# Off-diagonal attention values on four 32-column tiles in a hybrid convolution and forgetting-attention layer

## The reference

```python
# q, k, v: (B, S, 8 heads, 64); c = cumsum(log_sigmoid(forget logits))
s = jnp.einsum('bqhd,bkhd->bhqk', q_blk / 8, k)
s = s + c_q[..., :, None] - c_k[:, :, None, :]
s = jnp.where(causal, s, -jnp.inf)
pr = jax.nn.softmax(s, axis=-1)
y_attn = jnp.einsum('bhqk,bkhd->bqhd', pr, v)
```

## Time and profile before

| | |
|---|---|
| median of 3 runs | 4268.29 us (4263.36 to 4269.75) |
| the profiled execution | 4270.38 us |
| its slowest core (3), first to last instruction | 4268.8 us |
| spans of its eight cores | 4252.9 to 4268.8 us |
| mean granted TensorE clock of core 3 | 0.985 of full speed |
| TensorE busy / ScalarE busy / VectorE busy | 97% / 54% / 44% of the span |

### The profile page before, as it was taken

The page is one execution under the profiler, slowest core; times in us unless marked ns, Lnnn a source line. Parts: engine busy times, 40 slices in busy tenths (PEclk is TensorE's granted clock), DMA queues, the critical chain, the costliest instruction groups (busy, mean ns, idle before and its releaser), DMA issues.

```text
span 4268.8 us, 73847 instructions; the slowest of 8 cores (4252.9 to 4268.8 us)
## 1 busy us (share of the span) xinstructions
PE 4128.3 (97%) x23192; PEld 1673.9 (39%) x23192; DVE 1873.9 (44%) x3245; ACT 2293.5 (54%) x4028; POOL 282.9 (7%) x619
## 2 busy tenths in 40 slices
PE   6999899999999999999999999999999999999978
PEld 3444343443433333333444444444333333333333
DVE  4566554353443433424444453534434344343334
ACT  3525345464666666766334354645557566676621
POOL 1111000010000000000000000101001000000000
PEclk9999999999999999999999999999999999999989
DMA  8798965463543543624556473635436354352344
GB/s 193 148 186 205 197 191 158 121 191 116 155 144 108 160 126 110 175 90 150 174 165 183 133 203 123 194 122 167 145 114 190 102 153 139 98 162 95 99 141 124
DMA packets 350372, 635.10 MB, mean 149 GB/s; under 512 B 201648, under 2 KB 206000, under 8 KB 350000
## 3 DMA queue, kind: packets, MB, share of 16 engines
q1 hardware_dynamic: 333408, 585.89, 45.6%
q0 software_dynamic: 16592, 44.51, 6.9%
HBM read 567.84 MB, written 61.87 MB: 148 GB/s over the span
## 4 chain that ended last, share of the span: by engine, by line
PE 89%; DMA 4%; ACT 2%; issue 2%; DVE 2%; POOL 1%; SPq 0%; ACTq 0%; DVEq 0%; POOLq 0%
PE ps L1143 39%; PE ps L1327 14%; PE ps L1227 12%; PE ps L980 7%; PE ps L1037 6%; PE ps L1043 3%; PE ps L1072 2%; DMA xnC<-xnbf 2%; PE ps L989 1%; PE ps L1365 1%; DMA brow_s<-brow 1%; DMA xt<-x 1%; PE ps L986 1%; PE ps L1230 1%; ACT jk L669 1%
## 5 line engine op out<-in xcount | busy, mean ns | idle before, releaser
L1008 ACT ACTIVATE P<-ps,cKb 128x512 bf16<-128x512 f32 x1792 | 1105.7, 688 | 560.4 <-PE ps L980 558.0
L1143 PE MATMUL ps<-xnC,wslot 128*128 128x512 bf16 x5632 | 1288.7, 381 | 21.8 <-DMA xnC<-xnbf 11.8
L1143 PEld LDWEIGHTS ps<-xnC,wslot 128*128 128x128 bf16 x5632 | 533.4, 98 | 688.0 <-issue 98.2
L732 DVE TENSOR_TENSOR xt<-xt,ps 128x512 f32<-128x512 f32 x512 | 351.5, 687 | 661.6 <-PE ps L1327 489.3
L1327 PE MATMUL ps<-wslot,actT 128*128 128x512 bf16 x2816 | 637.2, 379 | 0.8 <-DVE actT L1189 0.8
L1143 PE MATMUL ps<-xnA,wslot 128*128 128x512 bf16 x2560 | 613.2, 389 | 0.3 <-DVE wslot L574 0.3
L1183 DVE SCALAR_TENSOR_TENSOR th<-th,ps 128x512 f32<-128x512 f32 x352 | 241.7, 687 | 681.2 <-ACT th L1181 670.0
L1181 ACT ACTIVATE th<-ps 128x512 f32<-128x512 f32 x352 | 210.6, 598 | 526.1 <-PE ps L1143 513.7
L1327 PEld LDWEIGHTS ps<-wslot,actT 128*128 128x128 bf16 x2816 | 266.6, 98 | 335.8 <-issue 35.3
L1008 ACT ACTIVATE P<-ps,lc 128x512 bf16<-128x512 f32 (+3 forms) x512 | 243.7, 526 | 283.2 <-PE ps L989 274.7
L980 PE MATMUL ps<-Q,KT 64*128 64x512 bf16 (+3 forms) x2304 | 360.8, 366 | 9.4 <-ACT P L1008 7.7
(11 more groups left out here) (114 smaller groups left out, 3144.9 us busy)
## 6 DMA issues: line engine op xcount, KB each, us to landing
wslot<-wst SPq DMA_DIRECT2D x773, 512.0 KB, 3.9
xt<-x SPq DMA_DIRECT2D x124, 512.0 KB, 6.7
wslot<-wpack POOLq DMA_DIRECT2D x75, 512.0 KB, 8.6
y<-xt SPq DMA_DIRECT2D x64, 512.0 KB, 7.4
wst<-wslot SPq DMA_DIRECT2D x53, 512.0 KB, 8.3
wslot<-wst SPq DMA_DIRECT2D x30, 256.0 KB, 2.6
pT<-pTd POOLq DMA_DIRECT2D x16, 256.0 KB, 10.9
xnC<-xnbf SPq DMA_TRANSPOSE x120, 4.4
```

The costliest lines, as they stand in the source:

```text
L732: yield Req("dve", lambda e: e.tensor_tensor(out=hh[:, dh * 512:(dh + 1) * 512], in0=hh[:, dh * 512:(dh + 1) * 512], in1=PS[b][:], op=ALU. ...
L1008: yield Req("act", lambda e, b=b, pi=pi, c0=c0, bias=bias: e.activation(out=Pb[pi][:, c0:T], in_=PS[b][:, c0:T], func=AF.Exp, bias=bias, s ...
L1143: ins = e.matmul(PS[b][:], lhsT=wv[:, kc, cols:cols + 128], rhs=xsrc[:, kc, :], start=(kc == 0), stop=(kc == 7))
```

## The change

The four value matmuls of a call of `fpv` become eight. Each head's 64 value dimensions are cut in two halves of 32 columns, and the eight products are written for the four 32-column tiles of the array, q = 0 to 3, as the row sums are: tiles 0 and 1 take the two halves of head 0, tiles 2 and 3 those of head 1, first for unit d = 0, then for d = 1. The PSUM bank and its layout stay what they were, and so does everything after it. The planner is told a cost of 0.68 in place of 0.77, and that the call begins and ends in shape C.

```diff
                         for d in range(2):
-                            for s_ in range(2):
-                                h = 2 * hp + s_
-                                e.matmul(PS[o_][64 * s_:64 * s_ + 64, :], lhsT=VA[:, kt + d, h * 64:(h + 1) * 64],
+                            for q in range(4):
+                                s_ = q // 2
+                                v0 = (2 * hp + s_) * 64 + 32 * (q % 2)
+                                e.matmul(PS[o_][32 * q:32 * q + 32, :], lhsT=VA[:, kt + d, v0:v0 + 32],
                                          rhs=Pb[2 * ((u + d) % NPU) + s_][:], start=(fi and d == 0),
-                                         stop=(la and d == 1))
+                                         stop=(la and d == 1), tile_position=(0, 32 * q))
...
                     if kp == 0:
-                        ob, lb = yield Req("pe", fpv, reads=rd, nb=2, grp="O", cost=0.77, mode=("B", "C"),
+                        ob, lb = yield Req("pe", fpv, reads=rd, nb=2, grp="O", cost=0.68, mode=("C", "C"),
                                            pen=lambda k=k, u=u: pv_pen(k, u))
                     else:
-                        yield Req("pe", fpv, reads=rd, writes=[Bps[ob], Bps[lb]], cost=0.77, mode=("B", "C"),
+                        yield Req("pe", fpv, reads=rd, writes=[Bps[ob], Bps[lb]], cost=0.68, mode=("C", "C"),
                                   pen=lambda k=k, u=u: pv_pen(k, u))
```

## The result

The changed kernel took 4220.5 and 4223.6 us, 4222.0 in the middle. The ratio to the kernel before is 0.9891, with a 95% interval of 0.9868 to 0.9915: 46.5 us faster, between 36 and 56. The prediction was 4218 us, 50 less than before.

A forecast was written before the change was run, and what follows sets the result against it. TensorE was taken to bound nearly everything; 55.1 us saved in calls less 2.1 for the order made 53.0, times 0.96 made 50.9, so 4270.4 became 4219.5, called 4218; range 4206 to 4240 for 8 in 10.

The forecast's parts named there:

- TensorE bounds it: Whole kernel: TensorE, busy 97% and 89% of the chain, bounds nearly everything, so time saved in fpv calls on the chain counts.
- The call: Each of 448 fpv calls: 0.762 us against 0.885, 0.123 less, 55.1 us in all.
- the shorter first pass: First value pass of a call: 32-column weights delay it 10 ns against 24, so 0.014 us less.
- Loads between C passes are hidden: Two boundaries inside each call, between passes of four 32-column tiles: weight loads hide behind the running pass, costing nothing.
- the rival that they are exposed: Two boundaries inside each call: weight loads of 92 ns each show, 29 us slower, 4298 us; chance 6%.
- The partly exposed rival: Same boundaries inside each call: 50 to 60 ns of loads show at each, 4260 to 4277 us, no change; chance 4%.
- Same-source tiles: Value passes: two tiles reading one P cost nothing; rival, they take turns, 193 us more, about 4410 us, chance 2%.
- Issue of instructions: A call's 24 loads and matmuls in place of 16: about 25 ns a pair, four pairs 100 ns, costed at nothing.
- Changes of shape in the new order: TensorE's order around the calls: 23 new changes of tile shape at 0.093 each, 2.1 us given back.
- The share that arrives: Calls' time on the chain: 96% of 53.0 us reaches the end, 50.9 us; the rest mostly in early slices.
- The planner's rival: TensorE's order: the new order makes TensorE wait for P, 19 us of 51 lost, 4237 us; chance 13%.

The follow-up runs named there:

- row-sum run: The kernel before, with the row sums on 64-column tiles like the values, in two passes and not one: 4310.3 us, ratio 1.0101.
- run with four sources: The changed kernel, with the four tiles of each value pass streaming four different P and not two: 4221.7 us, ratio 0.9886.
- diagonal run: The changed kernel's matmuls in the order of the kernel before, with the diagonal units' values and row sums also on four 32-column tiles: 4221.5 us, ratio 0.9888.
- run with the order alone: The kernel before with its 64-column value matmuls, but the planner's new cost and letters, so the changed kernel's order: 4275.7 us, ratio 1.0020.
- with the order kept: The changed kernel's eight value matmuls, but the planner's cost and letters, and so the order, of the kernel before: 4226.9 us, ratio 0.9897.

## Why the prediction was right, and where it was off

- **TensorE bounds it.** Right. With 1792 more matmuls and loads the time fell, since passes and changes of shape are what it pays for.
- **The call.** 0.762 was forecast and 0.764 measured; the second pass at 0.23 and the sums at 0.44 came as said. The change from 64 to 32 columns (0.10) and the shorter first pass (10 ns, not 24) are in the starts. It was worked out from the starts in one call, and the row-sum run priced the same terms from the other side, 987 ns against 984.
- **Loads between C passes are hidden.** Right, and the rival that they are exposed (4298) falls: the second pass came after 227 ns, not 300 or more. The partly exposed rival falls with it; its time was mis-added, since 50 to 60 ns a boundary give 4260 to 4269 and not 4277. The Trainium skill's page TensorE: Matmul & The Clock Gate, in Part 3 on packing small matmuls, lists that loads overlap matmuls only in another row group, though its paragraph on the mechanism also allows a background weight buffer; here four loads in the same row group ran under passes of 216 and of 56 ns, which goes against the first and leaves the second open.
- **Same-source tiles.** Right to cost at nothing; the run with four sources shows it.
- **Issue of instructions.** Costed at nothing, which holds, but the figure behind it was too high: 25 ns for a load and its matmul came from full-width loads with tiny matmuls. In the diagonal run four pairs start in 56 ns.
- **Changes of shape in the new order.** 2.1 us for 23 more; the run with the order alone has 3.3 us more on the core mean, 6.2 over all runs. This is consistent, no proof.
- **The share that arrives.** This step was mis-sized. I took 96% from the chain's rounded shares, which alone allow anything from 86% to all. The trace's own chain on that core holds 378 of the 396.5 us of the calls, 95%, so the reading was right by it; the rest is spread over the run, and not in the early slices, where I put it (12 of the 448 calls start in the first tenth). But with the order kept 85 to 87% of 54.2 us arrived (46.1 over all runs, 47.0 in the profiled ones), and in the changed kernel 79% (42.8 to 43). The share of the chain says how much lies on the path now, not what becomes late when the path gets shorter. In the other direction 88 to 93% of what the row-sum run added arrived.
- **How near the number came.** The forecast was 50 us less, and the slowest core gave 46.5; the mean of the cores, on which the terms were checked, gave 43. The slowest core stood some 10 us above the mean of the cores before and 7 now, over two runs. Part of the nearness is therefore luck.
- **The planner's rival.** Its kind of wait came, at a fraction of its price: 19 us were put against it. The order costs 3 to 6 us. Waits for P grew from 21.5 to 27.2 us on the mean of the cores, and with the old order they are 25.5 already; all waits together grew by 12.5, of which 8.3 appear with the old order as well. That they grow is shown; which of them cost the end, in each place, is not.

## What to carry to other kernels

Count TensorE's work in passes and in changes of tile shape, not in instructions: splitting a product into narrower tiles was free here, and leaving the array in one shape was worth about 0.09 to 0.10 us each time. So give neighbours the same shape, and then make the stretches between changes longer. Take a saving read off the chain as an upper bound: here 13 to 21% of what the calls gave up didn't reach the end. And compare a profiled execution with the other runs of its kernel before building on it: the one of the row-sum kernel stood 7 us off.

## What the runs showed of the hardware that I had not expected

- Two passes of four 32-column tiles, each with four weight loads and four matmuls, started 56 ns apart at 128 columns. Nothing of the loads shows; only the first pass after a change of shape waits, 10 ns with 32-column weights and 24 with 64-column ones.
- The same transposing DMA, issued 0.88 us after the start of the same scaling, landed after 5.4 us on the slowest core before and after 7.1 on that of the changed kernel, and TensorE's wait behind it followed.
- What changes inside the calls doesn't arrive whole: 54.2 us less gave 46, 45.7 us more gave 42.5, and a further 96.8 less gave 91.
